# Attention step: which engine multiplies the probabilities by the inverse sums in the first sixteen steps

## What is computed

```python
def row_block(r):
    ...
    s_loc = jnp.einsum('bchd,bacwhd->bhcaw', q_r, k_win).astype(jnp.float32)
    ...
    s_loc = (s_loc + bias[None].astype(jnp.float32)).reshape(B, H, GRID_W, n_loc)
    s_ctx = jnp.einsum('bchd,bnhd->bhcn', q_r, k_ctx).astype(jnp.float32)
    p = jax.nn.softmax(jnp.concatenate([s_loc, s_ctx], axis=-1), axis=-1).astype(v.dtype)
    ...
    return (jnp.einsum('bhcaw,bacwhd->bchd', p_loc, v_win)
            + jnp.einsum('bhcn,bnhd->bchd', p_ctx, v_ctx))
...
s = jnp.einsum('bnhd,bmhd->bhnm', qc, kc).astype(jnp.float32)
p = jax.nn.softmax(s, axis=-1).astype(vc.dtype)
att_c = jnp.einsum('bhnm,bmhd->bnhd', p, vc).reshape(B, N, D_A)
```

## Time and profile before

| | |
|---|---|
| median of 3 runs | 1605.69 us (1605.46 to 1607.34) |
| the profiled execution | 1607.11 us, of which the span of its instructions is 1605.3 us |
| busy over the span | PE 98%, PEld 86%, DVE 69%, ACT 45%, POOL 8% |
| granted TensorE clock | 0.997 of full speed |
| attention steps 0 to 15 | from about 114 us to 279 us of the span |

### The profile page before, as it was taken

How to read it: one execution, slowest core, us unless ns; L and a number is a source line. 1 busy time by engine, 2 the same in 40 slices (tenths; PEclk the granted TensorE clock), 3 DMA queues, 4 the chain that set the end, 5 groups by cost and what they waited for, 6 DMA issues and landing times.

```text
span 1605.3 us, 27507 instructions
## 1 busy us (share of the span) xinstructions
PE 1565.6 (98%) x10740; PEld 1380.9 (86%) x10740; DVE 1102.7 (69%) x1814; ACT 718.8 (45%) x1382; POOL 134.0 (8%) x184
## 2 busy tenths in 40 slices
PE   6999999999999999999999999999999999999999
PEld 5888777688899899899989977888888898989897
DVE  5798888543895388368638676777655876949675
ACT  4445455451742144124214353565683653626442
POOL 0434344010000000000000100101001000000000
PEclk9999999999999999999999999999999999999999
DMA  9632401552113221422331431111126223333233
GB/s 369 77 96 106 145 27 52 211 211 65 66 53 139 99 79 49 165 77 79 102 135 54 154 112 53 40 51 32 52 90 237 85 87 118 99 112 106 69 117 104
DMA packets 49513, 167.63 MB, mean 104 GB/s; under 512 B 5584, under 2 KB 5840, under 8 KB 49264
## 3 DMA queue, kind: packets, MB, share of 16 engines
q1 hardware_dynamic: 37104, 123.86, 23.4%
q10 hardware_dynamic: 7984, 28.31, 4.9%
q0 software_dynamic: 4304, 13.80, 2.9%
HBM read 161.72 MB, written 4.19 MB: 103 GB/s over the span
## 4 chain that ended last, share of the span: by engine, by line
PE 81%; DVE 8%; ACT 6%; DMA 2%; issue 2%; SPq 0%; ACTq 0%; DVEq 0%
PE PS L799 22%; PE PS L3148 8%; PE PS L2929 7%; PE PS L2704 6%; PE PS L2700 6%; PE PS L2701 6%; PE PS L2762 4%; PE PS L2766 4%; PE PS L2763 4%; PE PS L2771 2%; DVE c_early L2166 2%; DMA scr<-in_ada 1%; PE PS L2839 1%; PE PS L2662 1%; PE PS L2879 1%
## 5 line engine op out<-in xcount | busy, mean ns | idle before, releaser
L742 ACT ACTIVATE w_hi<-raw 128x1024 fp32r<-128x1024 f32 (+2 forms) x132 | 122.0, 926 | 202.6 <-PE PS L799 119.5
L1735 DVE SCALAR_TENSOR_TENSOR X<-PS,mod,X 128x512 f32<-128x512 f32 (+2 forms) x120 | 75.7, 659 | 193.7 <-PE PS L799 174.0
L799 PE MATMUL PS<-c_hi,w_hi 128*128 128x512 f32 x628 | 186.6, 355 | 2.8 <-DVE X L1735 2.0
L799 PE MATMUL PS<-c_lo,w_hi 128*128 128x512 f32 x628 | 184.8, 352 | 0.0
L748 DVE TENSOR_TENSOR w_lo<-raw,w_hi 128x1024 fp32r<-128x1024 f32 (+2 forms) x132 | 142.5, 1079 | 56.9 <-ACT w_hi L742 56.5
L799 PE MATMUL PS<-c_hi,w_lo 128*128 128x512 f32 x628 | 139.4, 352 | 0.0
L2166 DVE SCALAR_TENSOR_TENSOR c_early<-X,small,c_early 128x798 f32<-128x798 f32 x120 | 130.6, 1089 | 2.4
L799 PEld LDWEIGHTS PS<-c_hi,w_hi 128*128 128x128 f32 x628 | 102.4, 188 | 22.4 <-ACT w_hi L742 4.1
L799 PEld LDWEIGHTS PS<-c_lo,w_hi 128*128 128x128 f32 x628 | 102.1, 188 | 16.9
L799 PEld LDWEIGHTS PS<-c_hi,w_lo 128*128 128x128 f32 x628 | 102.1, 188 | 16.9
L2700 PE MATMUL PS<-h_hi,w_hi 128*128 128x384 f32 x320 | 107.4, 336 | 0.0
(11 more groups left out here) (471 smaller groups left out, 3832.5 us busy)
## 6 DMA issues: line engine op xcount, KB each, us to landing
raw<-in_w SPq DMA_DIRECT2D x108, 512.0 KB, 3.5
adaw<-in_w SPq DMA_DIRECT2D x40, 512.0 KB, 4.4
raw<-in_w SPq DMA_DIRECT2D x48, 384.0 KB, 3.1
adaw<-in_ada ACTq DMA_DIRECT2D x28, 512.0 KB, 4.4
scr<-in_ada POOLq DMA_DIRECT2D x19, 512.0 KB, 8.8
h_early<-in_ada SPq DMA_DIRECT2D x12, 512.0 KB, 5.2
scr<-in_ada ACTq DMA_DIRECT2D x12, 512.0 KB, 5.3
scr<-in_ada SPq DMA_DIRECT2D x4, 1024.0 KB, 14.0
```

The source lines that it names most:

```text
L742: nc.scalar.activation(w_hi[:, j, 0:tiles], raw[:, j].rearrange("p (k n) -> p k n", k=KT)[:, 0:tiles], ACT.Copy).then_inc(s_hi, 1)
L799: last = nc.tensor.matmul(G[j][:, a:b], w[:, j, k], m[:, k, a:b], start=(n == 1), stop=(n == 3 * k_tiles))
L1735: i = V.scalar_tensor_tensor(out=xs, in0=G[j][:, a:b], scalar=gv, in1=xs, op0=ALU.mult, op1=ALU.add)
```

## The change

POOL's function `scaled` goes, and ACT gets `probs_scaled`, which does the same multiplication as an activation with a scale operand: `ACT.Identity` with the inverse sum of each row as its scale, in place, one instruction for each head, the same 32 instructions over sixteen steps. It is called once ahead of the loop and then in step U for step U + 1. It stands behind the weight split for product b + 2 and ahead of `g_sigmoid`, the copy of product a, `attn_hi(U)` and the second weight split, and it waits for `s_rr` of step U + 1. POOL makes the masks of the four head pairs in a row, each still waiting for the maxima of the pair before. PE's and DVE's lists are the same, row for row.

```diff
-            def scaled(U):
-
-                nk = keys(U)
-                pool.wait_ge(s_rr, U + 1)
-                for h in (1, 0):
-                    p = Pb[:, U % 2, h, 0:nk]
-                    nc.gpsimd.tensor_tensor(p, p, tmp(3, U, h).to_broadcast([128, nk]), ALU.mult).then_inc(s_Ps, 1)
-
-            masks(0, (0, 1))
-            for U in range(SCALED):
-                scaled(U)
-                if U % 6 == 3:
-                    masks(U // 6 + 1, (0,))
-                if U % 6 == 4 or U == SCALED - 1:
-                    masks(U // 6 + 1, (1,))
+            for hp in range(4):
+                masks(hp, (0, 1))
...
+            def probs_scaled(U):
+
+                nk = keys(U)
+                act.wait_ge(s_rr, U + 1)
+                for h in (1, 0):
+                    p = Pb[:, U % 2, h, 0:nk]
+                    nc.scalar.activation(p, p, ACT.Identity, scale=tmp(3, U, h)).then_inc(s_Ps, 1)
+
...
             exponentials(0)
+            probs_scaled(0)
...
                 if b is not None:
                     split_next(b + 2)
+                if U + 1 < SCALED:
+                    probs_scaled(U + 1)
                 if kind_of(a1)[0] == "g":
                     g_sigmoid(a1)
                 ab_out(a)
```

## The result

Before: 1605.59 us, median of 6 executions (1605.20 to 1608.67). After: 1614.11 us, median of 6 (1610.45 to 1616.14), measured side by side. The ratio worked out from these executions is 1.004 with an interval of [1.003, 1.005], some 6.4 us; the two medians alone are 8.5 us apart. The direction is the forecast one and every step of it is found in the trace. The size is above the forecast of +4.1 us either way: by the ratio the time is 1605.69 x 1.004 = 1612.1 us, 2.3 above the forecast and just inside the range; the median of 1614.11 lies 4.3 above the forecast and 1.6 above the range. A term was missing.

A forecast was written before the change was run, and what follows sets the result against it. The prediction took PE, busy 160.1 of 166.0 us, as the bound; delays from ACT's queue less DVE's relief summed to +4.1 us on the median 1605.69, giving 1609.8 us, with a range from 1604.5 to 1612.5.

The forecast's parts named there:

- The bound and the place: PE nearly full between 113 and 279 us; changes on ACT and POOL count only where PE waits, 6.0 us together.
- The price: A pair on ACT delays what stands behind it by 1.24 us (512 columns), 1.13 (448) or 0.80 (256).
- Step 1: The pair delays ACT's copy of product 10, so PE starts product 11 later: +1.1 us.
- Step 5: ACT waits for the inverse, then scales, ahead of the sigmoid chain to PE's product 14: +2.0 us.
- Steps 7, 10 and 13: Pairs ahead of the copies of products 14, 16 and 18, less DVE's relief: +1.1, +0.4 and -0.1 us.
- Step 14: A k scaling on DVE gives back 0.4 us ahead of the last tap, where PE waits.
- Sum +4.1 us: PE's total delay from step 1 to the last convolution tap, all steps added.
- The rest of the program follows PE at the same distance: From step 16 on nothing is changed, so the delay stays as it is to the end.
- Swallowed delays: Rival: delays of steps 1 and 7 fall into PE's waits for products 16 and 18; +1.4, 1607.1 us; chance 0.25.
- Higher price: Rival: masks hinder DVE as the multiplications did, +6.7; with a pair at 1.4, +7.5, 1613.2 us; chance 0.12.
- Relief decides: Rival: from step 8 DVE, freed of POOL's multiplications, wins 3.5 us if ACT's pairs are hidden; 1602.2 us; chance 0.08.

The follow-up runs named there:

- e10: The changed kernel with useless PE matmuls filling the waits ahead of products 14 and 17, repeated on the third chip; 1613.08 us, 1.0033 of before.
- e4: The changed kernel with useless PE matmuls filling the waits ahead of products 14 and 17, on the first chip; 1610.91 us, 1.002 of before.
- e1: The changed kernel with ACT's pair of multiplications moved behind `attn_hi(U)`, ahead of the second weight split; 1604.06 us, 0.9983 of before.
- e12: The changed kernel with ACT's pair moved behind `attn_hi(U)`, repeated on another chip; 1603.52 us, 0.9975 of before.
- e8: The changed kernel without ACT's pairs, leaving out the multiplication by the inverse sums in the first sixteen steps; 1604.28 us, 0.9982 of before.
- e2: The changed kernel with the pair moved behind `attn_hi(U)` except in step 5, where it keeps its place; 1607.90 us, 1.0001 of before.
- e3: The changed kernel with the pair moved behind `attn_hi(U)` except in steps 1, 4, 7, 10 and 13; 1608.58 us, 1.0011 of before.
- e9: The changed kernel with useless PE matmuls filling the wait ahead of product 17 alone; 1612.62 us, 1.0033 of before.
- e11: The changed kernel as it is, run again on the third chip; 1612.70 us, 1.0034 of before.
- e6: The changed kernel with ACT's pair behind `attn_hi(U)` and POOL still multiplying, but its own table by ones; 1607.72 us, 1.0003 of before.

## Why the prediction was right, and where it fell short

**The bound and the place: right.** PE's waits were the right view: all steps of the forecast appear there, and nothing else did. No wait for the modulation weights of the earlier trace rows was added.

**The price: right.** The pairs in the changed kernel, groups of ACT, busy us, mean ns | idle before:

```profile
L1339 ACT ACTIVATE scr<-scr 128x512 f32<-128x512 f32 x12 | 8.0, 711 | 2.8 <-DVE scr L2210 2.8
...
L1339 ACT ACTIVATE scr<-scr 128x448 f32<-128x448 f32 x12 | 7.3, 658 | 3.3 <-DVE scr L2210 3.3
...
L1339 ACT ACTIVATE scr<-scr 128x256 f32<-128x256 f32 x8 | 3.6, 500 | 0.0
```

711, 658 and 500 ns against 709, 0.66 us and 499 taken from other lines. In step 1 the copy started 1.24 us after the pair, as forecast.

**Step 1: right.** Timeline of the changed kernel, answering to the earlier trace rows:

```profile
140.49 0.17 DVE L2210 RECIPROCAL scr<-scr 128x2 f32<-128x2 f32 x1 [0.54 <-ACT scr L1331]
...
140.69 1.34 ACT L1339 ACTIVATE scr<-scr 128x512 f32<-128x512 f32 x2 [0.23 <-DVE scr L2210]
...
141.93 1.07 ACT L1263 ACTIVATE scr<-PS 128x512 f32<-128x512 f32 x1
142.80 0.41 ACT L1265 ACTIVATE scr<-PS 128x256 f32<-128x256 f32 x1
...
143.36 0.58 PE L2927 MATMUL PS<-h_hi,w_hi 128*128 128x512 f32 x2 [0.96 <-ACT scr L1265]
```

The row gives 0.96 us of idleness, the table +1.0; forecast 1.1.

**Step 5: right, to the tenth.** 0.75 of waiting for the inverse and 1.23 for the pair make 1.98, and product 14 came 2.0 later.

**Steps 7, 10 and 13: right.** +1.0, +0.4, -0.1 against +1.1, +0.4, -0.1. **Step 14: half of it.** -0.2 against -0.4. PE's wait for the last tap was 0.3 us long, so no more than that could be won; of the steps it is the only one off by more than 0.1 us.

**The sum as a term of the whole: too small.** "Sum +4.1 us" is what the stretch costs where no fall of the clock lies in it: 3.9 in both traces with filled waits. What failed is a term that the sum put at nothing: PE's own pace behind the longer waits. The forecast lets products 14 and 17 run as fast as before; they ran 1.6 and 1.5 us longer in all three traces, at the lower clock. The profile of before gave no row for it: there PE waits 2.2 and 2.4 us and the clock stays at 1.00. Still, the same profile has 0.83 near 970 us, so that the clock can fall was to be seen, and the forecast lengthened one wait to 3.1 us without asking. "The rest of the program follows PE at the same distance" failed by less and the other way: from the last tap to the end the three traces win 1.2, 1.2 and 2.0 us back. That the ratio's 1612.1 lies inside the range is luck in part: the upper end, 1612.5, stands for a sum without any relief of DVE, and the relief was there.

How much of the excess in the medians that is can be bounded in another way. Over the 22 executions of the changed kernel whose clocks are listed the mean clock is 0.9951 and the mean time 1613.3 us; over 84 of the kernel before, 0.9969 and 1607.1. In both sets the time falls by 1.2 to 1.4 us for each 0.001 of clock. A line through each set gives 1610.7 and 1606.9 at 0.997, so at equal clock the change costs 3.8 us, the forecast sum within 0.3; the other 2.5 us go with the lower clock (0.0018 at 1.2 to 1.4 us per 0.001 is 2.2 to 2.5). The two filled runs fit: e10's mean time is 2.3 us above e4's, on another chip, and its clock 0.0021 lower. This is a fit, not an experiment, and it ties the excess to the clock, not to a wait. That it is the waits of products 14 and 17 is seen in three traces of three, and filling them removed the falls from the traces but not surely the time. That part stays open.

**The rivals.** *Swallowed delays* is out: products 11 and 15 are 1.0 us late each, and product 17's wait did not shrink, it grew from 2.2 to 2.6 us. *Higher price* would have come nearest to the median, for the wrong reason: taps took 1047 ns over the stretch with the masks running, so the masks did not hinder DVE as the multiplications had. *Relief decides* lost as the change is written, but its amount was near: the forecast put it at 3.5 us if the pairs were hidden, and e1, e12 and e8, where they are, show 2.7 to 3.8 by the medians.

## What to carry to other kernels

Moving work to a half-idle engine was decided here by its place in that engine's list, not by its load: with the same 32 instructions in front of copies that PE waits for the change cost 6 us, and with them behind, still a step ahead of their consumer, it won 3. Look for the first point in the list at which nothing queued behind is wanted soon, and for which wait the moved instruction brings along; here a wait for the inverse in front of two table loads. And when a change lengthens idle time on PE, put a price on the clock as well as on the wait.

## What the hardware showed that was not expected

A wait of PE in the midst of dense work can be followed by a stretch at the lower level of 1.2 GHz, and each such fall cost 1.3 to 1.6 us, about half of the wait in front of it or more. It is not tied to the length of one wait. Behind 3.1 us the clock fell in four of five traces (not in e2), behind 2.6 us in five of five, behind 2.1 to 2.4 us in some (e3, e9, e11) and not in others (both such waits of before, of e6), behind 1.7 us in e2 and e12 and not in e1 and e8. Nor does it need a wait: near 970 us it fell behind 24 small matmuls that took 2.85 us, with no wait above 0.5 us, in all traces but that of e12. What decides it in the single case stays open here.
